# Experts in steps of 768, 1024 and 1024 inner columns instead of 256 and five times 512

## The chip, the core and the metric

The kernel runs on one core of a Trainium2 chip. Its time is the device time of one launch in microseconds (us), the median of three runs. TensorE does the matmuls, with a weight load (LDWEIGHTS) ahead of each; ScalarE (ACT), VectorE (DVE) and GpSimd (POOL) do the elementwise work; SyncE (SP) issues the weight loads from HBM to SBUF.

## What is computed

Four layers over 256 tokens of width 1024, all in float32. The first two are attention layers with a plain MLP, the third an attention layer with a gated MLP. The fourth ends in a mixture of eight experts, and only the expert part of it is rewritten by the change. For each expert, with the rows of the tokens that the router sent to it (up to 128 at a time here):

```
y = (silu(x @ w_gate) * (x @ w_up)) @ w_down     # gate, up: 1024 x 2816; down: 2816 x 1024
```

y is weighted by the router's share and added to the token's row; a final norm follows. Two experts are taken per token. The weights of the eight experts are 277 MB.

## The kernel before

**Products in three passes.** Every weight tile is split into a high part and a low part so that a float32 product comes out of three faster ones (line 2351: high by high, 2352: high by low, 2353: low by high). A tile comes into a **raw slot** of `slab` by two DMAs of SyncE (`tile`, line 626). ScalarE rounds it to its high part in `w_hi` (`hi`, line 1892), VectorE subtracts to get the low part in `w_lo` (`lo`, line 977), and TensorE uses both. A tile is 128 partitions by 2048 columns, 1 MB, and serves 12 matmuls of 512 columns. In the experts there are six raw slots and three **split slots** (slots 1 to 3 of the four in `w_hi` and `w_lo`; slot 0 stays free for the end). SyncE waits, before it loads a raw slot again, for VectorE's subtraction of what was in it (semaphore `lo_dve`). ScalarE waits, before it writes a split slot again, for TensorE's last matmul on what was in it (`w_used`). All queues are in order, and the order on each engine is written out by hand.

**An expert** has 33 tiles. Its 2816 inner columns are taken in `MS` = 6 steps: one of 256 columns (`narrow`), in which gate and up lie side by side in two tiles, and five of 512 columns, with two tiles for up, two for gate and two for down each. Rows of a gate or up tile are 1024 or 2048 bytes in HBM, those of a down tile 4096. In step j TensorE computes up into PSUM bank 1 and gate into bank 0, then does the down matmuls of step j-1 into banks 2 and 3 (`sums`), then transposes the hidden block of step j (`turn`, line 2470; four 128-column transposes). In between ScalarE takes silu of the gate bank (line 2279), VectorE multiplies by up (line 1757), and after the transposes ScalarE and VectorE split the turned block (lines 2179 and 1559). The sums of an expert's last step come in the next expert's step 0. ScalarE then scales them (`output`), and GpSimd scatters them with an add into `y_rows` in HBM; GpSimd also fetches the rows of the next expert (`fetch`), which TensorE transposes (`turn_fetched`, line 2841), and VectorE builds the list of the expert after (`lists`, `make_index`; two small products on line 2834).

The first expert's body and the last one's are written out, and a loop runs three times over two experts each (`each_expert`). Steps 2 to 4 of an expert are an inner loop.

**Ahead of the experts** lies the output projection of layer 4: four tiles, number 13 to 16 of that layer, in split slots 1, 2, 3 and 0. On ScalarE's queue behind it come, in this order:

```
ring.stage(3 if l < MOE else MORE_RAW, 3, 1)     # raw slots, split slots, first split slot
loads0 = list(ring.loads)
hi()
if l == MOE:
    hi()
...
    square_halves()                              # four squares with sums, line 1923
```

`stage` keeps in `last` which tile was last in each split slot, and `hi` waits for TensorE's use of that tile. The projection's result is added to x in four pieces by VectorE (`add_gated`, lines 1073 and 1074), each followed by ScalarE's square of that piece; VectorE computes the means in `cross_gated`, in the order add, add, add, `first_half(0)`, `first_half(1)`, `mean(0)`, add(1, 1), scaled row, `mean(1)`, scaled row. The means wait for the squares (`ss_done`), and the fourth square for the fourth add. Norm, router and the first gather of rows follow one after another.

Of the kernel before, what the change touches and what calls it, by code (L numbers as in the profile page):

```python
# [17 lines left out]
P = 128  # L18
D = 1024
# [47 lines left out]
F_WIDE = 512  # L67
# [22 lines left out]
X_MACT, X_MACT2, X_G, X_YE = 4096, 4864, 4608, 5376  # L90
# [114 lines left out]
def build(nc, A, out):  # L205
    ctx = ExitStack()
    with ctx:
# [10 lines left out]
        hT_lo = sb("hT_lo", [P, KC, SEQ], F32R)  # L218
        big = sb("big", [P, ADA])
# [13 lines left out]
        posi = sb("posi", [P, TT], I32)  # L233
# [7 lines left out]
        flag = sb("flag", [1, 1], I32)  # L241
# [77 lines left out]
        last_g, rows_out, rows_in = sem("last_g"), sem("rows_out"), sem("rows_in")  # L319
# [29 lines left out]
        MT = 3 * MJ  # L349
        MS = 1 + (FF2 - F_GATED) // F_WIDE  # L350

# [3 lines left out]
        def ff_tiles(l):  # L355
            return 4 * steps(l) if l < DEPTH else MT
# [165 lines left out]
        def expert_ring(ring, i, p, t0, loads0, ahead=2):  # L522


            done = MT * p + ahead
            ring.t, ring.i, ring.raw, ring.split = t0 + i * (2 * MT) + done, done, MORE_RAW, 3
            ring.at = 0 if isinstance(i, int) and i == 0 and p == 0 and t0 == ring.start else -MORE_RAW
            ring.loads = [c + i * (2 * MT // MORE_RAW) + sum(k % MORE_RAW == s for k in range(done))
                          for s, c in enumerate(loads0)]
# [10 lines left out]
        def expert_steps(eng, ring, step, before_last):  # L540

            with eng.Fori(0, MS - 3) as jj:
                ring.enter(jj, 6)
                step(jj + 2)
            ring.leave(MS - 3)
            before_last()
            step(MS - 1)

        def narrow(j):

            return isinstance(j, int) and j == 0

        def wide_at(j):

            return j * F_WIDE - F_GATED

        def expert_after(t0, loads0):

            return t0 + NE * MT, [c + NE * MT // MORE_RAW for c in loads0]
# [19 lines left out]
        def listed(p, b):  # L579

            return slice(KC // 2 * p + 2 * b, KC // 2 * p + 2 * b + 2)
# [5 lines left out]
        def by_two(src):  # L587

            return src.rearrange("p (a n) -> p a n", a=2)
# [4 lines left out]
        def _(sp):  # L594
# [82 lines left out]
            for l in LAYERS:  # L677
# [57 lines left out]
                else:  # L735
                    stage(MORE_RAW)

                    def expert_loads(t0, loads0, n0):
# [5 lines left out]
                        def body(i, p, n, first, last):  # L744
                            wg, wu, wd = weights(2 * i + p)
                            expert_ring(ring, i, p, t0, loads0)

                            def step(j, norm=False):
                                cols(wu, wide_at(j + 1), F_WIDE)
                                if norm:  # L750

                                    sp.wait_ge(sc_done, 2 * (UNIT0[l] + UNITS[l]))
                                cols(wg, wide_at(j + 1), F_WIDE)
                                if narrow(j):
                                    rows(wd, 0, 1)
                                else:
                                    rows(wd, 4 * j - 2, 2)

                            def final(j):
                                if not last:  # L760
                                    gated(*weights(2 * i + p + 1)[:2], 0)
                                rows(wd, 4 * j - 2, 2)

                            step(0, first and n0 == 0)
                            step(1)
                            if first and n0 == 0:
# [4 lines left out]
                            expert_steps(sp, ring, lambda j: final(j) if isinstance(j, int) else step(j), lambda: None)  # L771

                        ring.t, ring.i, ring.loads = t0, 0, list(loads0)
                        ring.at = 0 if t0 == ring.start else -MORE_RAW
                        gated(*weights(0)[:2], 0)
                        each_expert(sp, n0, body)

                    t0, loads0 = ring.t, list(ring.loads)
                    expert_loads(t0, loads0, 0)
# [3 lines left out]
                    with sp.If(full > P + 1):  # L783
                        expert_loads(*expert_after(t0, loads0), NE)
# [7 lines left out]
        def _(pool):  # L792
# [22 lines left out]
            with nc.allow_non_contiguous_dma(reason="256 positions"):  # L815
                pool.dma_start(posi[:, :].unsqueeze(2), A["positions_2"].rearrange("a (t p) -> p t a", p=P)).then_inc(v_in, 16)
# [92 lines left out]
            def clear_sums():  # L909

                pool.dma_start(y_rows.rearrange("(a p) d -> p a d", p=P), big[:, 0:D].unsqueeze(1).broadcast_to([P, TT + 1, D])
                               ).then_inc(scattered, 16)

            def fetch(p, n, n0):
# [3 lines left out]
                pool.indirect_dma_start(fetched, None, h_rows, bass.IndirectOffsetOnAxis(index[p][:, 0:1], 0)).then_inc(rows_in, 16)  # L918

            def scatter(p, n, n0):  # L920

                pool.wait_ge(yo_done, 2 * (n - n0 // NE) + 2)
                pool.wait_ge(scattered, 16 * (n + 1))
                pool.indirect_dma_start(y_rows, bass.IndirectOffsetOnAxis(index[p][:, 0:1], 0), y_out, None, compute_op=ALU.add  # L924
                                        ).then_inc(scattered, 16)

            def sums_back(turn_):

                pool.wait_ge(scattered, 16 * NE * (turn_ + 1))
                pool.dma_start(acc, y_rows[0:SEQ].rearrange("(t p) d -> p t d", p=P)).then_inc(acc_in, 16)  # L930

            def expert_rows(n0):

                for n in range(n0, n0 + NE):
                    p = n % 2
                    if n > n0:
                        scatter(1 - p, n - 1, n0)
                    if n < n0 + NE - 1:
                        fetch(1 - p, n + 1, n0)
# [4 lines left out]
            pool.wait_ge(rows_out, 32)  # L944
# [13 lines left out]
        def _(dve):  # L958
# [174 lines left out]
            def tables():  # L1133

                dve.wait_ge(v_in, 16 * V_LOADS)
                link(dve.tensor_copy(posf[:, :], posi[:, :]))
# [79 lines left out]
            for l in LAYERS:  # L1216
# [325 lines left out]
                if l >= DEPTH:  # L1542
                    ring.stage(3 if l < MOE else MORE_RAW, 3, 1)
# [152 lines left out]
                def matches(e, signal):  # L1696

                    pe_ = pos[:, :, bass.ds(e, 1)]
                    for t in range(TT):
                        dve.tensor_scalar(scr(X_G + t * P, P), iota, pe_[:, t], None, ALU.is_equal).then_inc(signal, 1)  # L1700

                def lists(e, n):
# [4 lines left out]
                    matches(e, g_done)  # L1707
# [12 lines left out]
                def last_lists(n):  # L1720

                    dve.wait_ge(ix_t, n + 1)
                    matches(NE - 1, last_g)

                def make_index(p, n, old):

                    dve.wait_ge(ix_t, n + 1)
                    if old:
                        dve.wait_ge(scattered, 16 * n)
# [1235 lines left out]
```

## Time and profile before

| what | value |
|---|---|
| median of the runs | 1911.68 us (1910.37, 1911.68, 1918.38) |
| span of the profiled execution | 1912.1 us, 0.4 us above the median |
| TensorE, ScalarE, VectorE busy | 1824.1, 1122.6, 1416.6 us |
| mean granted clock of TensorE | 0.983 of full speed |
| first expert's first matmul | 1142.61 us |
| last matmul on expert weights | 1896.70 us |
| DMA in the experts | about 381 GB/s |

The page names no time of the profiled execution apart from its span; the span is within the scatter of the runs and is taken as its own time. A matmul's duration in the rows is longer than the distance to the next one, since matmuls overlap; the pace is read from the starts. The clock is given as a share of 2.4 GHz: 1.00 is 2.4 GHz and 0.50 is 1.2 GHz.

### The profile page before, as it was taken

What the parts mean: (1) busy time and instruction counts of PE and PEld (TensorE: products, weight loads), DVE (VectorE), ACT (ScalarE), POOL (GpSimd) and SP (SyncE); (2) the same over time, 40 slices, a digit from 0 to 9 for tenths busy, and PEclk for the clock granted to TensorE, in tenths of its full rate; (3) what the DMA queues carried; (4) which work ended last, traced back from release to release, by engine and by line L of the source; (5) the groups of instructions that cost most, each with busy time, mean ns of one, the idle gap of its engine ahead of it and who ended that gap; (6) DMA issues with size and microseconds to landing.
All of it is one profiled execution on the core that took longest, in us unless ns stands there. A gap on an engine that the chain in (4) does not pass through costs nothing.

```text
span 1912.1 us, 26024 instructions
## 1 busy us (share of the span) xinstructions
PE 1824.1 (95%) x8799; PEld 1486.2 (78%) x8799; DVE 1416.6 (74%) x1631; ACT 1122.6 (59%) x1296; POOL 392.8 (21%) x315
## 2 busy tenths in 40 slices
PE   7899999989999998899989879999999999999997
PEld 6678886868888786688878667888888888888885
DVE  5748874466976586644458758889888888888897
ACT  6745444564443464443345537777777777777775
POOL 3722203463212363200046500000000000000000
PEclk9999999999999999999999989999999999999999
DMA  8348884418987341455544258999999999999994
GB/s 271 111 161 327 343 342 147 149 54 323 344 347 275 91 152 45 154 195 179 192 154 142 69 187 334 386 376 386 380 384 376 383 383 381 380 374 381 381 387 167
DMA packets 237934, 506.45 MB, mean 265 GB/s; under 512 B 23304, under 2 KB 74720, under 8 KB 231712
## 3 DMA queue, kind: packets, MB, share of 16 engines
q1 hardware_dynamic: 225664, 492.91, 70.9%
q0 software_dynamic: 3008, 10.32, 2.0%
q10 hardware_dynamic: 9184, 2.23, 0.5%
q8 instruction: 43, 0.70, 0.1%
q14 instruction: 35, 0.29, 0.0%
HBM read 497.49 MB, written 7.91 MB: 264 GB/s over the span
## 4 chain that ended last, share of the span: by engine, by line
PE 83%; DVE 7%; issue 6%; ACT 3%; POOL 1%; DMA 0%; POOLq 0%; SPq 0%; DVEq 0%; ACTq 0%
PE bank L2351 25%; PE bank L2353 25%; PE bank L2352 25%; PE bank L2470 2%; ACT slab L2042 1%; PE bank L2789 1%; DVE slab L1290 1%; PE bank L2561 1%; PE bank L2539 1%; ACT w_hi L1892 1%; PE bank L2521 1%; POOL w_lo L826 1%; DVE x L1074 0%; PE bank L2572 0%; DVE slab L1271 0%
## 5 line engine op out<-in xcount | busy, mean ns | idle before, releaser
L977 DVE TENSOR_TENSOR w_lo<-slab,w_hi 128x2048 fp32r<-128x2048 f32 x369 | 847.8, 2308 | 214.3 <-ACT w_hi L1892 213.3
L1892 ACT ACTIVATE w_hi<-slab 128x2048 fp32r<-128x2048 f32 (+2 forms) x421 | 796.6, 1898 | 329.0 <-PE bank L2353 256.3
L2351 PE MATMUL bank<-w_hi,hT_hi 128*128 128x512 f32 (+3 forms) x1664 | 649.4, 390 | 14.2 <-DVE hT_lo L1012 4.4
L2352 PE MATMUL bank<-w_lo,hT_hi 128*128 128x512 f32 (+3 forms) x1664 | 638.0, 383 | 0.0
L2353 PE MATMUL bank<-w_hi,hT_lo 128*128 128x512 f32 (+3 forms) x1664 | 637.9, 383 | 0.0
L2351 PEld LDWEIGHTS bank<-w_hi,hT_hi 128*128 128x128 f32 x1664 | 316.0, 190 | 77.9 <-DVE w_lo L977 8.8
L2353 PEld LDWEIGHTS bank<-w_hi,hT_lo 128*128 128x128 f32 x1664 | 315.5, 190 | 59.7
L2352 PEld LDWEIGHTS bank<-w_lo,hT_hi 128*128 128x128 f32 x1664 | 316.3, 190 | 55.3
L826 POOL TENSOR_TENSOR w_lo<-slab,w_hi 128x512 fp32r<-128x512 f32 (+2 forms) x208 | 262.4, 1295 | 381.3 <-ACT w_hi L1892 361.6
L2351 PE MATMUL bank<-w_hi,hid_hi 128*128 128x512 f32 x680 | 265.6, 391 | 0.7 <-DVE w_lo L977 0.7
L2353 PE MATMUL bank<-w_hi,hid_lo 128*128 128x512 f32 x680 | 265.0, 390 | 0.0
L2352 PE MATMUL bank<-w_lo,hid_hi 128*128 128x512 f32 x680 | 264.5, 389 | 0.0
L2351 PEld LDWEIGHTS bank<-w_hi,hid_hi 128*128 128x128 f32 x680 | 127.6, 188 | 29.2 <-issue 2.3
L2353 PEld LDWEIGHTS bank<-w_hi,hid_lo 128*128 128x128 f32 x680 | 127.6, 188 | 26.7
L2352 PEld LDWEIGHTS bank<-w_lo,hid_hi 128*128 128x128 f32 x680 | 127.7, 188 | 26.3
L924 POOL DMA_INDIRECT y_rows<-slab,posi x7 | 16.6, 2367 | 515.6 <-ACT slab L2263 515.6
L901 POOL TENSOR_TENSOR slab<-slab 128x512 f32<-128x512 f32 x32 | 60.0, 1893 | 251.6 <-ACT slab L2188 251.6
L1577 DVE SCALAR_TENSOR_TENSOR big<-slab,csilu,big 128x2048 f32<-128x2048 f32 x42 | 103.5, 2473 | 0.0
L2042 ACT ACTIVATE slab<-slab,att 128x256 f32<-128x256 f32 x144 | 71.4, 499 | 52.3 <-DVE att L1271 43.0
L2179 ACT ACTIVATE hid_hi<-bank 128x512 fp32r<-128x512 f32 (+1 forms) x95 | 47.6, 527 | 46.1 <-PE bank L2470 46.1
L1290 DVE TENSOR_TENSOR slab<-slab,att 128x512 f32<-128x512 f32 x56 | 52.7, 942 | 5.8
L1271 DVE CUSTOM_DVE_ANT_0 slab<-bank,const 128x256 f32<-128x256 f32 x88 | 31.9, 417 | 33.4 <-PE bank L2521 33.3
(252 smaller groups left out, 1232.0 us busy)
## 6 DMA issues: line engine op xcount, KB each, us to landing
slab<-in_w_exp_gate SPq DMA_DIRECT2D x176, 512.0 KB, 7.0
slab<-in_w_exp_up SPq DMA_DIRECT2D x176, 512.0 KB, 7.5
slab<-in_w_exp_down SPq DMA_DIRECT2D x176, 512.0 KB, 7.1
slab<-in_w_ada SPq DMA_DIRECT2D x48, 1024.0 KB, 5.5
slab<-in_w_mlp_in SPq DMA_DIRECT2D x64, 512.0 KB, 5.4
slab<-in_w_mlp_out SPq DMA_DIRECT2D x64, 512.0 KB, 9.0
slab<-in_w_in SPq DMA_DIRECT2D x56, 512.0 KB, 5.0
slab<-in_w_out SPq DMA_DIRECT2D x32, 512.0 KB, 4.6
```

The source lines that it names most:

```text
L826: ins = pool.tensor_tensor(w_lo[:, q, o], raw(s)[:, o], w_hi[:, q, o].bitcast(F32), ALU.subtract)
L901: pool.tensor_tensor(scr(X_ACT2 + t * F_UP, F_UP), a, a, ALU.mult).then_inc(sq_done, 1)
L977: dve.tensor_tensor(w_lo[:, q, 0:n], raw(s)[:, 0:n], w_hi[:, q, 0:n].bitcast(F32), ALU.subtract).then_inc(lo_dve, 1)
L1290: dve.tensor_tensor(p, p, r[:, s, :].unsqueeze(2).broadcast_to([P, TT, SEQ]), ALU.mult).then_inc(nrm_done, 2)
L1577: ins = dve.scalar_tensor_tensor(acc, w, c, acc, ALU.mult, ALU.add)
L1892: act.activation(w_hi[:, q, 0:n], raw(s)[:, 0:n], ACT.Copy).then_inc(hi_done, 1)
L2042: act.activation(p, p, ACT.Exp, bias=att[:, 1, j, t:t + 1], scale=-1.0, accum_out=att[:, 2, j, t:t + 1]).then_inc(ex_done, 1)
L2179: act.activation(to_hi[:, f0:f0 + n, t * P:(t + 1) * P], src, ACT.Copy).then_inc(hidh_done, 1)
L2351: pe.matmul(dst, a_hi, b_hi, start=start, stop=False)
L2352: pe.matmul(dst, a_hi, b_lo, start=False, stop=False)
L2353: return pe.matmul(dst, a_lo, b_hi, start=False, stop=stop_)
L2470: ins = pe.transpose(dst[t][:, f * P:(f + 1) * P], scr(src + t * width_ + f * P, P), ident)
```

## The change

The 2816 inner columns are taken in `MS` = 3 steps of 768, 1024 and 1024. Gate goes to banks 0 and 1, up to banks 4 and 5 (half of the step's columns in each bank, so 384 or 512 columns a matmul). A gate or up tile is now two rows of k by the whole step: 2 x 768 or 2 x 1024 columns, in HBM rows of 3072 or 4096 bytes. There are 36 tiles in an expert instead of 33: eight of 1536 columns, two of 1024 (the last two chunks of step 0's six down chunks), and 26 of 2048. TensorE's order within an expert is up and gate of step 0, down of the last expert's step 2, turn 0, up 1, gate 1, down 0, turn 1, up 2, gate 2, the turn of the fetched rows, down 1, turn 2. In the first expert up 1 comes ahead of turn 0 and uses banks 6 and 7. The split slots are all four, tile r in slot r % 4. Silu and the multiplication of a step are two instructions each, as are the two splits of the turned block. The inner loop is gone, the outer one stays. The list is in a part of scratch of its own, `hT_hi` and `hT_lo` each hold one expert's rows with high and low parts, the clearing of `y_rows` is three DMAs instead of one, and the waits count from constants instead of from the `Tiles` bookkeeping.

The core of the diff:

```
+E_WIDTH = (768, 1024, 1024)
+E_FROM = (0, 768, 1792)
+MS = len(E_WIDTH)
+MT = 36
...
+        def up_tile(j, first):
+            return (0 if first else -4, 8, 20)[j]
+        def gate_tile(j, first):
+            return (4 if first else 0, 12, 24)[j]
+        def down_tile(j):
+            return (4, 16, 28, MT - 4)[j + 1]
+        def tile_width(r, first, last):
+            if r in (18, 19):
+                return D
+            return 2 * E_WIDTH[0] if r < 4 or first and r < 8 or r >= MT - 4 and not last else TILE
...
+                        def wide_rows(w, j, n, r0):
+                            for b in range(4):
+                                to, loaded = slot_free(n, r0 + b)
+                                d = to[:, 0:2 * E_WIDTH[j]].rearrange("p (k n) -> p k n", k=2)
+                                for k in range(2):
+                                    sp.dma_start(d[:, k:k + 1, :], w[:, 2 * b + k:2 * b + k + 1, E_FROM[j]:E_FROM[j] + E_WIDTH[j]]
+                                                 ).then_inc(loaded, 16)
```

VectorE's queue in an expert:

```
+                        lows(2 if first else -1, gate_tile(0, first) + 7)
+                        activated(0)
+                        if first:
+                            lows(11, 15)
+                        else:
+                            lows(7, 11)
+                        hidden_low(0)
+                        if not last:
+                            lists(2 * i + p + 1, n + 1)
+                        lows(15 if first else 11, 19)
+                        activated(1)
+                        lows(19, 23)
+                        hidden_low(1)
...
+                            lows(23, 31)
+                        activated(2)
```

ScalarE ahead of the experts, and its rounding of a tile:

```
-                    ring.stage(3 if l < MOE else MORE_RAW, 3, 1)
+                    ring.stage(*((3, 3, 1) if l < MOE else (MORE_RAW, SPLIT, 0)))
                     loads0 = list(ring.loads)
-                    hi()
+                    hi(2 * E_WIDTH[0] if l == MOE else TILE)
                     if l == MOE:
-                        hi()
+                        hi(2 * E_WIDTH[0])
...
+                            def highs(r0, r1):
+                                for r in range(r0, r1):
+                                    w, s, q = tile_width(r, first, last), raw_slot(r), split_slot(r)
+                                    act.wait_ge(w_loaded[s], n * (32 * MT // MORE_RAW) + 32 * (loads0[s] + r // MORE_RAW + 1))
...
+                                    act.activation(w_hi[:, q, 0:w], raw(s)[:, 0:w], ACT.Copy).then_inc(hi_done, 1)
```

TensorE's queue in an expert:

```
+                        inner(0)
+                        gate(0)
+                        if first:
+                            inner(1)
+                            pe.wait_ge(ix_made, 2 * n + 2)
+                            turn(0)
+                        else:
+                            sums(-1)
+                            turn(0)
+                            inner(1)
+                        gate(1)
...
+                        sums(0)
+                        turn(1)
```

ScalarE's `highs`, silus and copies lie in the same places of its queue as VectorE's `lows`, `activated` and `hidden_low`. In the last expert four instructions that fold the scattered sums into x stand between VectorE's `lows` of tiles 24 to 28; before they stood between those of steps 3 and 4.

## Rows read from the trace of the kernel before

**Rows 1.** Busy time by stretch: each engine's us (instructions), granted clock, DMA share, GB/s.

```profile
1142.60:1146.80 4.20, 4.19 (x11) 3.33 (x12) 2.56 (x4) 2.21 (x2) 0.00 (x0) 0.60 0.14 53
...
1155.00:1217.00 62.00, 62.00 (x286) 51.40 (x285) 55.94 (x37) 44.81 (x29) 3.03 (x1) 1.00 1.02 381
1217.05:1310.78 93.73, 93.73 (x432) 77.76 (x431) 83.82 (x54) 70.63 (x49) 3.40 (x2) 1.00 1.04 381
...
1796.30:1896.90 100.60, 99.91 (x450) 81.15 (x448) 90.37 (x55) 70.85 (x50) 3.15 (x2) 1.00 0.88 328
```

**Rows 2.** Waits, 1200 to 1850 us: engine line <- awaited, us in total, times, longest.

```profile
ACT w_hi L1892 <- PE bank L2353: 93.2, 146, 1.2
```

**Rows 3.** Waits of SyncE's queue in the same stretch.

```profile
SPq L626 <- DVE w_lo L977: 375.0, 229, 3.1
```

**Rows 4.** Chain of work, 1100 to 1912 us: start, us, what.

```profile
1166.18 0.34 PE bank L2834 x4
...
1217.05 0.87 PE bank L2841 x8
...
1310.78 0.87 PE bank L2841 x8
```

**Rows 5.** TensorE in time order, 512-column matmuls: start, duration, line.

```profile
1293.14 0.39 PE L2353 MATMUL bank<-w_hi,hid_lo 128*128 128x512 f32 x1
...
1298.39 0.39 PE L2353 MATMUL bank<-w_hi,hT_lo 128*128 128x512 f32 x1
...
1309.95 0.39 PE L2353 MATMUL bank<-w_hi,hid_lo 128*128 128x512 f32 x1
```

**Rows 6.** TensorE in time order, 384-column matmuls of a projection.

```profile
712.42 0.33 PE L2351 MATMUL bank<-w_hi,hT_hi 128*128 128x384 f32 x1
...
715.71 0.33 PE L2352 MATMUL bank<-w_lo,hT_hi 128*128 128x384 f32 x1
```

**Rows 7.** ScalarE groups by form, whole run: busy us, mean ns.

```profile
L1892 ACT ACTIVATE w_hi<-slab 128x2048 fp32r<-128x2048 f32 x405 | 774.2, 1917 | 325.3 <-PE bank L2353 252.6 <-DMA slab<-in_w_mlp_in 55.9 <-DMA slab<-in_w_in 6.2
...
L1892 ACT ACTIVATE w_hi<-slab 128x1536 fp32r<-128x1536 f32 x12 | 17.6, 1488 | 0.0
```

**Rows 8.** Groups by form, 1280 to 1912 us: busy us, mean ns.

```profile
L977 DVE TENSOR_TENSOR w_lo<-slab,w_hi 128x2048 fp32r<-128x2048 f32 x216 | 492.6, 2291 | 62.8 <-ACT w_hi L1892 62.0 <-issue 0.3
...
L1757 DVE TENSOR_TENSOR slab<-slab,bank 128x512 f32<-128x512 f32 x33 | 22.5, 681 | 0.7
...
L2279 ACT ACTIVATE slab<-bank 128x512 f32<-128x512 f32 x33 | 19.8, 599 | 20.4 <-PE bank L2353 20.4
...
L1713 DVE TENSOR_TENSOR big<-big,rowg 128x1024 f32<-128x1024 f32 x2 | 2.4, 1218 | 0.0
```

**Rows 9.** The SyncE loads of line 626, 1217 to 1311 us: time from issue to landing.

```profile
DMA to landing us min/median/max: 4.9/7.6/9.8
```

**Rows 10.** ScalarE in time order, from the last projection to the first expert.

```profile
1096.62 1.90 ACT L1892 ACTIVATE w_hi<-slab 128x2048 fp32r<-128x2048 f32 x1
1103.40 1.92 ACT L1892 ACTIVATE w_hi<-slab 128x2048 fp32r<-128x2048 f32 x1 [4.88 <-PE bank L2353]
1110.31 0.63 ACT L1923 ACTIVATE h<-x 128x512 f32<-128x512 f32 x1 [4.99 <-DVE x L1074]
...
1115.67 0.63 ACT L1923 ACTIVATE h<-x 128x512 f32<-128x512 f32 x1 [1.99 <-DVE x L1074]
```

**Rows 11.** VectorE in time order, the last update of x.

```profile
1114.22 0.69 DVE L1073 TENSOR_TENSOR slab<-bank,rowg 128x512 f32<-128x512 f32 x1 [0.22 <-PE bank L2353]
1114.95 0.69 DVE L1074 TENSOR_TENSOR x<-slab,x 128x512 f32<-128x512 f32 x1
```

**Rows 12.** TensorE's last matmul of the output projection.

```profile
1113.80 0.39 PE L2353 MATMUL bank<-w_hi,hT_lo 128*128 128x512 f32 x1
```

**Rows 13.** TensorE in time order, its two waits in the first expert.

```profile
1150.90 0.44 PE L2470 MATMUL bank<-const,slab 128*128 128x128 f32 x2 [0.93 <-DVE slab L1757]
...
1154.57 0.50 PE L2351 MATMUL bank<-w_hi,hT_hi 128*128 128x512 f32 x1 [0.48 <-DVE w_lo L977]
```

More of the change, by code:

```diff
@@ L520, in build @@
         g_tables = rowg[:, 0:8 * HD].rearrange("p (a t d) -> p a t d", a=4, t=TT)
[L522 to L529, printed above, removed]
+        mact, mact2 = scr(X_MACT, max(E_WIDTH)), big[:, B_MACT2:B_MACT2 + max(E_WIDTH)]
+        EXPERT0 = FF0[MOE]
+        EXPERT_LO = FREE_RAW + EXPERT0 - len(POOLED)
         def each_expert(eng, n0, body):
@@ L742, in weights, with slot_free @@
                                     for n in ("w_exp_gate_2", "w_exp_up_2", "w_exp_down_2")]
[L744 to L766, printed above, removed]
+                        def slot_free(n, r):
+                            at = MT * n + r - MORE_RAW
+                            if at >= 0:
+                                sp.wait_ge(lo_dve, EXPERT_LO + at + 1)
+                            return raw(raw_slot(r)), w_loaded[raw_slot(r)]
@@ new lines, in expert_loads @@
+                        before = None
+                        for n in range(n0, n0 + NE):
+                            first, last = n == n0, n == n0 + NE - 1
+                            wg, wu, wd = weights(n - n0)
+                            wide_rows(wu, 0, n, up_tile(0, first))
+                            if n == 0:
+                                sp.wait_ge(sc_done, 2 * (UNIT0[l] + UNITS[l]))
+                            wide_rows(wg, 0, n, gate_tile(0, first))
+                            if not first:
+                                down_rows(before, -1, n)
+                            wide_rows(wu, 1, n, up_tile(1, first))
+                            wide_rows(wg, 1, n, gate_tile(1, first))
+                            down_rows(wd, 0, n)
+                            if n == 0:
@@ L770, in body @@
                                              ).then_inc(gfin_in, 16)
[L771 to L779, printed above, removed]
+                            wide_rows(wu, 2, n, up_tile(2, first))
+                            wide_rows(wg, 2, n, gate_tile(2, first))
+                            down_rows(wd, 1, n)
+                            if last:
+                                down_rows(wd, 2, n)
+                            before = wd
+                    expert_loads(0)
                     nrow += 1
@@ new lines, in activated @@
+                        def activated(j):
+                            at = ub + n * (2 * MS) + 2 * j
+                            banks = (bank[6], bank[7]) if first and j == 1 else (bank[4], bank[5])
+                            w = half_of(j)
+                            for c, o in enumerate(halves(j)):
+                                dve.wait_ge(act_done, at + c + 1)
+                                dve.tensor_tensor(mact2[:, o], mact[:, o], banks[c][:, 0:w], ALU.mult).then_inc(sq_done, 1)
@@ new lines, in turn @@
+                        def turn(j):
+                            nf = inner_chunks(j)
+                            banks = (bank[2], bank[3]) if first and j == 0 else (bank[0], bank[1])
+                            for f in range(nf):
+                                if f % (nf // 2) == 0:
+                                    pe.wait_ge(sq_done, ub + n * (2 * MS) + 2 * j + f // (nf // 2) + 1)
+                                src = mact2[:, f * P:(f + 1) * P]
+                                ins = pe.transpose(banks[f // 4][:, f % 4 * P:(f % 4 + 1) * P], src, ident)
+                            ins.then_inc(ht_done, 1)
```

421 lines of the change are left out of this document (225 added, 196 removed).

## The prediction

> **What bounds the kernel now.** I read the busy times by stretch first. In a whole expert, from one turn of fetched rows to the next, TensorE is busy 93.73 of 93.73 us at a granted clock of 1.00; VectorE is busy 83.82 us and ScalarE 70.63 [rows 1]. The chain of work has that turn at 1217.05 and again at 1310.78 us, so an expert costs TensorE's time to the hundredth [rows 4]. The DMA share of 1.04 looks like a second bound, so I read the waits: SyncE stands 375.0 us waiting for VectorE to free raw slots [rows 3], and ScalarE waits for TensorE to free split slots, 93.2 us in 650, never for a landing [rows 2]. A queue that is held back by its consumer is not what holds the consumer. TensorE sets the pace; the rest has to keep up.
>
> Next I took TensorE's pace apart. From 1298.39 to 1309.95 us there are 51 steps of 512 columns: 0.2267 us each [rows 5]. From 712.42 to 715.71 us there are 19 steps of 384 columns: 0.1732 us each, their weight loads included [rows 6]. The difference is 53.5 ns for 128 columns, 0.418 ns a column, so 12.6 ns of each matmul do not depend on its width. A transpose costs 0.87 / 8 = 0.109 us [rows 4]. From 1293.14 to 1298.39 us lie four transposes and 21 matmul steps: 5.25 - 21 x 0.2267 = 0.49 us, of which 0.44 are the transposes, so a break in the stream of matmuls costs 0.05 us beside its content [rows 5]. Check: 396 x 0.2267 + 30 transposes x 0.109 + 0.34 for the list [rows 4] + 6 breaks x 0.05 = 93.7 us, the period that was measured.
>
> **What the change does to an expert.** The columns stay the same. Step 0's up and gate are now 8 x 2 x 2 x 3 = 96 matmuls of 384 columns; the same work was 72 of 512. So 96 x 0.1732 - 72 x 0.2267 = 16.63 - 16.32 = +0.30 us. The turns go from six to three with the same 22 transposes; the fetched rows' turn, which adjoined a turn, now stands alone. Breaks go from six to four: -0.11 us. Together +0.19 us an expert, +1.5 us in eight.
>
> The rows put 12.6 ns on a matmul whatever its width. The Trainium skill ("TensorE: Matmul & The Clock Gate", Back-to-back issue gap) gives N/2.4 + 2.5 ns for an isolated warm matmul, 215.8 ns at 512 columns; the trace does not agree, with 226.7 ns. By its 2.5 ns the 24 extra matmuls would cost 0.06 us an expert and the sum would be 1.9 us lower.
>
> **Do the others still keep up?** Low parts first. A 1536-column subtraction has no row; between 1218 ns at 1024 and 2291 ns at 2048 columns [rows 8] I take 1755. VectorE then has 26 x 2.291 + 8 x 1.755 + 2 x 1.218 = 76.0 us in place of 33 x 2.291 = 75.6. On ScalarE 1488 ns at 1536 and 1917 at 2048 [rows 7] give about 1060 at 1024: 26 x 1.917 + 8 x 1.488 + 2 x 1.06 = 63.9 in place of 63.3. Products, copies and splits keep their number. Half a us more on engines with 10 and 23 us to spare costs nothing while their place in the queue is right, which has to be looked at apart.
>
> With three split slots a rounding starts when the tile three back is used, and its low part is there 1.92 + 2.29 = 4.2 us later, 1.2 us ahead of 2 x 2.72 us of matmuls (a tile is 12 x 0.2267 = 2.72 us). With four slots it is 8.2 - 4.2 = 4.0 us ahead. This margin pays for the longer interruptions. The tightest place in an ordinary expert is tile 23. Count from the end of tile 15: TensorE reaches tile 23 after 2 x 2.72 + 2 x 1.36 (the short down tiles) + 0.87 (eight transposes) + 0.34 (list) + 3 x 2.72 = 17.5 us. Rounding 21 starts when 17 is used, at 5.4; the low part of 21 is ready at 9.8, of 22 at 12.1; then the two halves of hidden_low, 1.36 by line 1757's 681 ns [rows 8]; the index, about 0.5; and tile 23 ends at 16.2. It is 1.3 us early. If it were late by d, d is paid in seven experts. In the last expert four folds of 1.22 us lie between tiles 24 and 28 and eat 4 x (1.22 + 2.29 - 2.72) = 3.2 us, so a wait of 1 to 2 us is due there; the last expert of before idles about as much (100.60 us against 99.91 busy, with slowed restarts) [rows 1]. I take zero, with 1.5 us both ways.
>
> Loads: slot r is loaded after the low part of tile r - 6. In the narrow stretch six tiles last 6 x 12 x 0.1732 = 12.5 us, rounding and subtraction 3.2, which leaves 9.2 us for a landing and 2.0 us of lead behind it: 11.2 us. Landings took 4.9 to 9.8 us, median 7.6 [rows 9]. Before it was 16.3 - 4.2 + 1.2 = 13.3. So nothing is paid, with a thinner margin. The fetch of the next expert's rows follows the index, at 13.9 us in the count above, and its turn comes behind gate 2, at 17.5 + 5 x 2.72 = 31.1; GpSimd's queue keeps its order and is 17 us early. The short DMAs of 256 and 384 KB and the six extra issues an expert lie in SyncE's waiting time [rows 3].
>
> **The first expert.** Before, TensorE waits 0.93 us for the product behind its first silu, with nothing else in the queue, and then 0.48 us for a low part whose rounding stood behind that silu [rows 13]. Now eight tiles and up 1 come before turn 0, and ScalarE rounds nine tiles before its first silu. TensorE has 10.9 us of matmuls over the silu (0.60 us each [rows 8]) even with a table load ahead. -1.4 us. If tiles 8 to 11 come late, because only six tiles of 1536 columns are in the raw slots at the start, up to 1 us of it stays.
>
> **The moved slot.** This is the largest term, and it is not in the experts. Expert tile 0 used to go into split slot 1, last used by projection tile 13; it now goes into slot 0, last used by tile 16, the final one. Before, ScalarE did the two roundings at 1096.62 and 1103.40 us, and was at the first square at 1110.31 [rows 10]. Now the first rounding waits for the last matmul of the projection, which starts at 1113.80 and takes 0.39 us [rows 12]: 1114.2. Everything queued behind it waits: rounding 0, rounding 1 (1.49 each [rows 7], less some 0.1 of overlap), then the squares from about 1117.0. VectorE waits for square 0 in `first_half(0)`, and behind that stand `mean(0)` and the fourth add. Three squares of 0.63 [rows 10] with about 0.1 each for reading out the sum end at 1119.2, `mean(0)` at 1119.4; the fourth add takes 1.42 us (1114.22 to 1115.64 [rows 11]) and ends at 1120.9; the fourth square starts there instead of at 1115.67 [rows 10]. That is +5.2 us on norm, router, gather and the first matmul, which follow one by one with no cover. From both sides: nothing, if something between the square and the gather waits for another thing; 6.8 us, if all four squares shift with the first (1110.31 to 1117.0).
>
> **Sum.** 1912.1 + 5.2 - 1.4 + 1.5 = 1917.4 us of span; against the median, 0.4 lower, 1917.0.
>
> **Rivals.**
> *The moved slot costs nothing* (chance 0.15). It needs an earlier release of slot 0 than I read. For: the rounding is only preparation. Against: the waits are in one queue ahead of the squares. Then 1917.0 - 5.2 = 1911.8.
> *The feed falls short in the narrow stretch* (0.18, slower). Eight tiles of 1536 columns fill six slots with a quarter less. For: the margin falls from 13.3 to 11.2 us, and the DMA share is already 1.04. Against: no landing of rows 9 was over 9.8. At 13.5 us each of seven experts pays 2.3 us: 1917 + 16 = 1933. It decides over slower by 0.5% from a landing of 11.8 us, 0.6 us an expert. Late low parts at tile 23 would look the same. The Trainium skill ("DMA: Bandwidth & Descriptors", Bandwidth) speaks for this rival with its rule to batch DMAs to 1 MiB; this trace moves 381 GB/s with DMAs of 512 KB, so the rule does not bind here before.
> *TensorE's clock falls once more* (0.05): TensorE now stands idle 5 us longer before the router. A stretch such as 1142.60 to 1146.80, at 0.60 granted, loses about 2 us over its matmuls [rows 1]: 1919, or 1921 with two.
> *Longer rows pay* (0.04, faster). If landings, not TensorE, set the pace in part, rows of 3072 and 4096 bytes would save time. TensorE's 93.73 of 93.73 speaks against it [rows 1]; a saving of 1.5 us an expert without the slot's cost gives 1900.
>
> **How the numbers follow.** The likeliest (0.58) has its own range of 1913 to 1921: the last expert 1.5 both ways, the start up to 1, the shift up to 6.8. To hold 8 in 10 the range goes down to 1909, over most of the first rival, and up to 1926, over the clock and the nearer part of the feed rival; beyond lie about 0.12 above and 0.06 below. A measurement of this kernel tells about 0.5% (9.6 us) from no change, so same is 1902 to 1921: 0.58 + 0.15 + 0.04 = 0.77. Slower, from the feed rival and a double clock loss, 0.18. Faster 0.05.
>
> **What would show it.** In the profile after: the rounding before the squares starts at about 1114.2 us on a wait for TensorE, the fourth square at about 1121, the first expert's matmul at about 1147.8; no wait of TensorE at its first turn; a period of 93.9 us between fetched turns with TensorE wholly busy; last expert as long as before within 1.5 us. The prediction is wrong if ScalarE shows waits for DMA in the experts, if TensorE waits for low parts in each expert, or if the squares start near 1110.

## The result, and the profile after

The changed kernel takes 1926.21 us (median of 4 runs, 1924.58 to 1927.95) against 1911.39 us: a ratio of 1.0067, 95% interval 1.0044 to 1.0089. Timed a second time it took 1922.2 against 1911.65, 1.0053 [1.0034, 1.0072]. It is slower both times. 1917.0 had been forecast, with a range of 1909 to 1926 and most of the chance given to a change within 0.5%: the first measurement lies 0.2 us above the range, the second inside it.

The head of its page:

```profile
span 1923.3 us, 25162 instructions
## 1 busy us (share of the span) xinstructions
PE 1830.4 (95%) x8991; PEld 1517.4 (79%) x8991; DVE 1415.1 (74%) x1653; ACT 1125.2 (59%) x1320; POOL 396.3 (21%) x317
```

The time of this profiled execution is named beside its span: 1925.05 us, 1.8 us more. By the same 1.8 us the profiled execution of before stood near 1913.9, some 2.5 us over the median of 1911.39, while this one stands 1.2 under its own. So of the 14.8 us between the medians the two traces show 11.2, the distance of the spans; the other 3.6 are scatter of single executions.

The chain of work shows the turns of the fetched rows, one an expert, which answer to [rows 4] (start, us, what):

```profile
1218.79 0.87 PE bank L2939 x8
1312.77 0.87 PE bank L2939 x8
1406.78 0.87 PE bank L2939 x8
1419.43 2.60 issue
1505.19 0.87 PE bank L2939 x8
1599.20 0.87 PE bank L2939 x8
1611.85 2.09 issue
1697.10 0.87 PE bank L2939 x8
1791.11 0.87 PE bank L2939 x8
```

Four of the six periods are 93.98 to 94.01 us. The other two are 98.41 and 97.90 us, and each of these holds a stretch in which TensorE waited for nothing that the profile shows. Busy time by stretch (first expert; ordinary; a long one; the last one; columns as in [rows 1]):

```profile
1146.53:1218.79 72.26, 72.26 (x344) 63.11 (x345) 63.74 (x46) 54.55 (x38) 2.27 (x1) 0.98 0.98 381
1218.79:1312.77 93.98, 93.98 (x456) 81.00 (x455) 83.60 (x57) 70.94 (x52) 4.45 (x2) 1.00 0.99 379
1406.78:1505.19 98.41, 95.81 (x456) 82.59 (x455) 83.76 (x57) 71.05 (x52) 4.39 (x2) 0.98 0.97 365
1791.11:1907.40 116.29, 116.26 (x555) 99.23 (x554) 102.67 (x65) 82.86 (x63) 2.39 (x2) 1.00 0.87 333
```

The long period has the same work (x456), 2.60 us idle and 1.8 us more of busy time. TensorE in time order there:

```profile
1418.39 1.04 PE L3019 MATMUL bank<-const,big 128*128 128x128 f32 x8
1422.03 0.44 PE L2453 MATMUL bank<-w_hi,hT_lo 128*128 128x384 f32 x1 [2.60 <-issue]
...
1423.00 0.33 PE L2455 MATMUL bank<-w_hi,hT_lo 128*128 128x384 f32 x1
...
1423.68 0.52 PE L2455 MATMUL bank<-w_hi,hT_lo 128*128 128x384 f32 x1
1424.00 0.52 PE L2453 MATMUL bank<-w_hi,hT_lo 128*128 128x384 f32 x1
```

The eight transposes are `turn(2)`, the last thing in the loop's body, and the 384-column matmul behind the wait is the first thing in it. So the wait is the branch back; three rounds have two of these. What is waited for there the trace doesn't name; the runs below show it. A microsecond and a half behind the wait the matmuls go from a pace of 0.173 us to 0.320, the pace of the clock's lower level, for ten of them: 10 x 0.147 = 1.5 us.

ScalarE ahead of the experts, which answers to [rows 10]:

```profile
1114.38 2.85 ACT L1958 ACTIVATE w_hi<-slab 128x1536 fp32r<-128x1536 f32 x2 [17.43 <-PE bank L2455]
1117.14 0.61 ACT L1989 ACTIVATE h<-x 128x512 f32<-128x512 f32 x1
...
1120.74 0.63 ACT L1989 ACTIVATE h<-x 128x512 f32<-128x512 f32 x1 [1.68 <-DVE x L1120]
```

Both roundings wait for the projection's last matmul, and the fourth square starts at 1120.74 instead of 1115.67. The waits in the experts of the changed kernel, 1200 to 1850 us (engine line <- awaited, us in total, times, longest):

```profile
ACT w_hi L2345 <- PE bank L2455: 117.8, 163, 3.4
...
PE bank L2453 <- issue: 4.7, 2, 2.6
ACT w_hi L2345 <- DMA slab<-in_w_exp_gate: 4.1, 3, 1.9
ACT w_hi L2345 <- DMA slab<-in_w_exp_down: 3.4, 5, 0.8
...
ACT w_hi L2345 <- DMA slab<-in_w_exp_up: 1.9, 3, 0.6
```

ScalarE now waits 9.4 us for landings, where [rows 2] had none, but TensorE's only waits are the two at the branch.

**Where the time went**, from trace to trace (first matmul on expert weights 1142.61 to 1146.53, last one 1896.70 to 1907.40): start +3.9; first expert, from its first matmul to the fetched turn, 74.44 to 72.26, -2.2; six periods 562.39 to 572.32, +9.9, of which 8.3 are the two branches (4.4 and 3.9 over the 94.0 of the others) and 1.6 the six times 0.27 of the others; from the last fetched turn to the last weight matmul 117.26 to 116.29, -1.0; behind it +0.5. Together +11.1, the spans differ by 11.2.

### The profile page after: what moved, and what is told of

Same layout as the page of the kernel before. It is cut to its first block, busy times and chain, and to the rows that moved or that the text cites. A ratio compares the mean times of both kernels' runs of the same rounds, so it can differ in the third digit from the quotient of the medians.

```text
span 1923.3 us, 25162 instructions
## 1 busy us (share of the span) xinstructions
PE 1830.4 (95%) x8991; PEld 1517.4 (79%) x8991; DVE 1415.1 (74%) x1653; ACT 1125.2 (59%) x1320; POOL 396.3 (21%) x317
## 4 chain that ended last, share of the span: by engine, by line
PE 83%; DVE 6%; issue 6%; ACT 3%; POOL 1%; DMA 0%; POOLq 0%; SPq 0%; DVEq 0%; ACTq 0%
PE bank L2453 25%; PE bank L2455 25%; PE bank L2454 25%; ACT slab L2108 1%; PE bank L2887 1%; DVE slab L1336 1%; PE bank L2568 1%; PE bank L2659 1%; PE bank L2637 1%; PE bank L3019 1%; ACT w_hi L1958 1%; PE bank L2619 1%; POOL w_lo L870 1%; PE bank L2670 0%; DVE x L1120 0%
## 5 line engine op out<-in xcount | busy, mean ns | idle before, releaser
L1788 DVE TENSOR_TENSOR w_lo<-slab,w_hi 128x2048 fp32r<-128x2048 f32 (+2 forms) x286 | 595.7, 2115 | 69.3 <-ACT w_hi L2345 66.7
L2453 PE MATMUL bank<-w_hi,hT_hi 128*128 128x512 f32 (+2 forms) x1352 | 516.9, 382 | 12.6 <-DVE hT_lo L1072 3.8
L2454 PE MATMUL bank<-w_lo,hT_hi 128*128 128x512 f32 (+2 forms) x1352 | 509.7, 377 | 0.0
L2455 PE MATMUL bank<-w_hi,hT_lo 128*128 128x512 f32 (+3 forms) x1336 | 503.7, 377 | 0.0
L1023 DVE TENSOR_TENSOR w_lo<-slab,w_hi 128x2048 fp32r<-128x2048 f32 x105 | 246.1, 2354 | 136.3 <-ACT w_hi L1958 136.3
L2454 PEld LDWEIGHTS bank<-w_lo,hT_hi 128*128 128x128 f32 x1352 | 257.7, 191 | 39.2
L2455 PEld LDWEIGHTS bank<-w_hi,hT_lo 128*128 128x128 f32 x1336 | 254.9, 191 | 41.1
L2455 PE MATMUL bank<-w_hi,hT_hi 128*128 128x512 f32 (+1 forms) x400 | 149.4, 374 | 0.0
L2453 PE MATMUL bank<-w_hi,hT_lo 128*128 128x512 f32 (+1 forms) x384 | 144.9, 377 | 4.7 <-issue 4.7
L2454 PE MATMUL bank<-w_lo,hT_lo 128*128 128x512 f32 (+1 forms) x384 | 143.7, 374 | 0.0
```

Source lines behind the costliest of these rows:

```text
L1023: dve.tensor_tensor(w_lo[:, q, 0:n], raw(s)[:, 0:n], w_hi[:, q, 0:n].bitcast(F32), ALU.subtract).then_inc(lo_dve, 1)
L1788: dve.tensor_tensor(w_lo[:, q, 0:w], raw(s)[:, 0:w], w_hi[:, q, 0:w].bitcast(F32), ALU.subtract).then_inc(lo_dve, 1)
L2453: pe.matmul(dst, a_hi, b_hi, start=start, stop=False)
L2454: pe.matmul(dst, a_hi, b_lo, start=False, stop=False)
L2455: return pe.matmul(dst, a_lo, b_hi, start=False, stop=stop_)
```

## The experiments

In the table, periods are those between fetched turns; "long" are the two with a branch. Ratios are to the kernel before on the same chip; its medians there were 1910.87 to 1911.68 us. The first matmul moves by several us between executions of code that is the same up to it ("both": 1142.65 and 1147.63), so it is read together with the distances inside a trace.

| run | median us | ratio [95%] | first expert matmul | periods, short; long |
|---|---|---|---|---|
| before | 1911.39 | | 1142.61 | 93.73; none |
| after | 1926.21 | 1.0067 [1.0044, 1.0089] | 1146.53 | 94.00; 98.41, 97.90 |
| after, again | 1922.2 | 1.0053 [1.0034, 1.0072] | 1147.81 | 94.00; 99.26, 96.41 |
| slot moved back | 1916.26 | 1.0025 [1.0013, 1.0037] | 1144.33 | 94.00; 96.31, 96.07 |
| loop written out | 1917.17 | 1.0030 [1.0018, 1.0042] | 1146.18 | 94.00; none |
| both | 1910.52 | 0.9996 [0.9981, 1.0012] | 1142.65 | 94.00; none |
| both, again | 1912.14 | 1.0002 [0.9989, 1.0015] | 1147.63 | 94.00; none |
| before, long body | 1927.27 | 1.0082 [1.0064, 1.0100] | 1147.40 | 93.73; 99.49, 98.71 |
| before, half long | 1911.21 | 0.9992 [0.9981, 1.0004] | 1139.78 | 93.74; none |
| before, slot moved | 1917.21 | 1.0019 [1.0004, 1.0035] | 1146.42 | 93.73; none |
| three slots, written out | 1922.51 | 1.0057 [1.0036, 1.0078] | 1142.34 | 95.25; none |
| both, short rows | 1913.84 | 1.0007 [0.9994, 1.0020] | 1140.12 | 94.00; none |
| both, step 0 packed | 1909.58 | 0.9992 [0.9981, 1.0003] | 1140.38 | 93.65; none |

**The slot moved back, in the changed kernel** (slot 1 first, as before; still four slots):

```
-            return r % SPLIT
+            return (r + 1) % SPLIT
-    ring.stage(... (MORE_RAW, SPLIT, 0) ...)      # in three places, and FREE_SLOT 0 -> 1
+    ring.stage(... (MORE_RAW, SPLIT, 1) ...)
```

> The changed kernel with its expert tiles in split slot (r + 1) % 4, so that the first tile follows projection tile 13 as before. If the moved slot is what delayed the start, ScalarE is at the first square near 1110.3 us again, the fourth square comes at about 1115.7 instead of 1120.7, and TensorE's first expert matmul at about 1142.6 instead of 1146.5: 3.9 us less, about 1922 us. If the late start has another cause (the order of the gather, the longer bodies), the first matmul stays near 1146.5 and the time near 1926. The long periods (98.4 and 97.9 us) should stay in either case.

ScalarE in time order:

```profile
1104.89 1.49 ACT L1958 ACTIVATE w_hi<-slab 128x1536 fp32r<-128x1536 f32 x1 [5.42 <-PE bank L2455]
1111.79 0.63 ACT L1989 ACTIVATE h<-x 128x512 f32<-128x512 f32 x1 [5.42 <-DVE x L1120]
...
1117.16 0.63 ACT L1989 ACTIVATE h<-x 128x512 f32<-128x512 f32 x1 [1.99 <-DVE x L1120]
```

The squares follow the additions again. This execution was about 1.5 us late already at the roundings (1104.89 against 1103.40), so the distance counts: from the projection's end to the first expert matmul 29.0 us, 28.8 before and 32.6 in the changed kernel. The time fell further than expected, to 1916.26: 5.9 us under the changed kernel's second measurement and 10.0 under its first. The branches are still there, as waits of 2.06 and 1.83 us, this time without a clock drop behind them:

```profile
1417.24 2.06 issue
...
1607.56 1.83 issue
```

**TensorE's loop over pairs of experts written out, in the changed kernel:**

```
-                    each_expert(pe, n0, body)
+                    for e in range(NE):
+                        body(e // 2, e % 2, n0 + e, e == 0, e == NE - 1)
```

> The changed kernel with TensorE's loop over pairs of experts written out, so that TensorE never branches back; the other engines keep their loops. If the waits of 2.6 and 2.1 us at 1419 and 1612 us are TensorE fetching the code it branches back to, both go, and the slow matmuls behind them: all periods 94.0 us, 8.3 us less, about 1918 us. If they come from another engine's loop or from data (the lists, the rows of the next expert), both stay and the time stays near 1926.

The fetched turns on both sides of the former first branch:

```profile
1406.44 0.87 PE bank L2939 x8
1500.42 0.87 PE bank L2939 x8
```

No wait for issue is left and all periods are 93.98 to 94.01; the median, 1917.17, is the expected one. The late start stays (fourth square 1120.40, 32.6 us from the projection's end to the first expert matmul).

**Both edits together.**

> Both edits in one kernel. If the two are the whole loss but for the narrower matmuls: 1926.2 - 3.9 - 8.3 = 1914, that is 2 to 3 us above the kernel before less what the first expert gains. If the edits don't add up, or something else was also slow, it stays above 1918.

> The kernel of e3_both again beside the other two, as their measure: 1910.5 us.

The kernel is level with the one before, twice, and some 3 us under the 1914 that was expected: the changed kernel's first median, from which that was worked out, was high. By the medians the slot costs 6.7 us (1917.17 less 1910.52) and the two branches 5.7 (1916.26 less 1910.52). Their sum over 1910.52 is 1922.9, which is what the changed kernel took the second time; the first time it took 3.3 more. This difference was not settled. The price of the branches varies from execution to execution (below), but it is not shown that this is the cause.

**The kernel before, with its inner loop written out** in TensorE's queue. The work is the same; the body of the outer loop grows from 504 matmuls on weights (the inner body counted once) to 792, each with its weight load:

```
-                        with pe.Fori(0, MS - 3) as j:
-                            ring.enter(j, 6)
+                        for j in range(MS - 3):
                             rows_up(j + 2)
                             sums(n, j + 1, False, False)
                             turn(j + 2)
```

> The kernel before, with TensorE's inner loop over steps 2 to 4 of an expert written out, so that the body of its outer loop has as many matmuls as in the changed kernel (396 an expert instead of 252), and nothing else changed. If the length of the code that is branched over makes the wait, two periods between fetched turns grow from 93.7 to about 98 us and the time rises by about 8 us to 1919. If the wait belongs to the new order of TensorE's work (only a short turn ahead of the branch) or to another engine, nothing changes: 1911.

TensorE in time order at the first branch:

```profile
1424.79 0.60 PE L2470 MATMUL bank<-const,slab 128*128 128x128 f32 x4
1429.27 0.50 PE L2351 MATMUL bank<-w_hi,hT_hi 128*128 128x512 f32 x1 [3.88 <-issue]
...
1430.28 0.63 PE L2352 MATMUL bank<-w_lo,hT_hi 128*128 128x512 f32 x1
1430.71 0.63 PE L2353 MATMUL bank<-w_hi,hT_lo 128*128 128x512 f32 x1
```

The wait appears in the kernel before, at 3.88 and 3.40 us, with a stretch at the lower clock behind it; the two periods are 5.8 and 5.0 us long. That is 10.7 of the 16 us that it lost. From trace to trace the rest is small: the first fetched turn comes 3.2 us later (1220.25 against 1217.05), and 3.2 + 10.7 is about the 13.7 between the spans (1925.8 against 1912.1). But 8 us had been expected, and all four executions lost 13.4 us or more against the median before. If the branches cost 10.7 us in each of them, 3 us or more are open.

**The same for one expert of the two**, a body of 648 matmuls on weights.

> The kernel before, with TensorE's inner loop written out for one of the two experts in the outer loop's body: 252 + 396 matmuls in it, between the 504 of before (no wait) and the 792 that waited. If TensorE keeps a fixed amount of code at hand and this still fits, the periods stay 93.73 us and the time 1911; if it doesn't, two periods are 4 to 6 us longer and the time is about 1920. Either way it tells where the limit lies. If instead the written-out loop itself were slow, each odd period would be longer.

No wait and no loss. So it is not the branch that costs but the length of what is branched over. With other engines' queues and the work the same, the limit lies between 648 and 792 matmuls with their weight loads; the changed kernel has 840. The DMA queue that carries instructions shows the same. Its lines for 1400 to 1800 us (packets, MB, share), first half long (before has the same line word for word), then long body, changed kernel, and changed kernel with the loop written out:

```profile
q8 instruction: 1, 0.02, 0.0%
```

```profile
q8 instruction: 19, 0.31, 0.3%
```

```profile
q8 instruction: 18, 0.29, 0.3%
```

```profile
q8 instruction: 16, 0.26, 0.3%
```

The line names no engine, but between before and the long body only TensorE's queue differs. A body that fits is hardly fetched again; one that doesn't is fetched all through, 16 KB at a time (0.29 MB in 18 packets, one in 22 us). The last line keeps one from reading too much into the packets: code without a branch back is fetched nearly as often, 16 packets, and TensorE waits for none of them. Only the fetch at the branch is waited for.

The Trainium skill ("Runtime: NRT & Kernel Launch", Instruction fetch mechanics) states the rule: instructions come in blocks of 16 KiB, 256 to a block, and a taken branch whose target is not in the window held at the moment waits for a fetch by DMA. The packets and the waits at the branch agree. It gives that window as two blocks, and TensorE's memory as 2048 instructions. With 648 matmuls and 648 loads a body of more than five blocks branches back for nothing, so two blocks is not the window of this engine; 792 and 792, 1584 instructions beside the transposes and register operations, miss it. More exactly the limit was not looked for.

**The kernel before, with the moved slot alone:** three split slots 0 to 2 instead of 1 to 3.

```
-    ring.stage(3 if l < MOE else MORE_RAW, 3, 1)
+    ring.stage(*((3, 3, 1) if l < MOE else (MORE_RAW, 3, 0)))       # in three places, and FREE_SLOT 0 -> 3
```

> The kernel before, with its expert tiles in split slots 0 to 2 instead of 1 to 3 (the free slot is then 3) and nothing else changed. The first tile then follows the projection's last tile. If the moved slot alone costs the late start, the first square is at about 1117 us, the fourth at about 1121, the first expert matmul 4 to 5 us later and the time 4 to 5 us longer, about 1915. If the cost needed the new experts as well, nothing changes.

```profile
1113.42 3.71 ACT L1892 ACTIVATE w_hi<-slab 128x2048 fp32r<-128x2048 f32 x2 [17.42 <-PE bank L2353]
...
1120.64 0.63 ACT L1923 ACTIVATE h<-x 128x512 f32<-128x512 f32 x1 [1.68 <-DVE x L1074]
```

ScalarE's rows are those of the changed kernel. The fourth square is 5.0 us late, the first expert matmul 3.8 (1146.42 against 1142.61). The median rose by 5.6 us; the ratio, 1.0019, stands for 3.6, with an interval of 0.8 to 6.7.

**The changed kernel again,** beside the last two.

> The changed kernel as it is, on the same chip as these: 1926 us as before, two periods between fetched turns of about 98 us. It is the measure for the other runs.

It took 1922.2 us where 1926 had been expected. The two waits are 3.42 and 2.15 us; behind the first 1.8 us more went to the lower clock, behind the second 0.3.

**Three split slots in place of four**, in the changed kernel with its loop written out:

```
-            return r % SPLIT
+            return 1 + r % 3          # and the counts of used slots: 3 in place of SPLIT
```

> The changed kernel with TensorE's loop written out, the first tile in slot 1, and three split slots (1 to 3) instead of four. By the margins worked out in the prediction a full tile is then ready 1.2 us before TensorE wants it, and two products or two splits in a row (1.36 us) use that up: TensorE should wait for low parts some tenths at several places of every expert, 1 to 2 us an expert, and the time should be 1919 to 1925. If four slots are more than it needs, the periods stay at 94.0 us and the time at 1911.

```profile
1243.94 0.47 PE L2453 MATMUL bank<-w_hi,hid_hi 128*128 128x512 f32 x1 [0.26 <-DVE w_lo L1788]
```

A period is 95.25 us (1214.15 to 1309.40 in the chain), 1.25 more: TensorE waits for low parts a few tenths at a time. Half of that is idle time (TensorE is busy 94.59 of the 95.25 us), the other half slower starts behind the waits: the same work takes 93.98 us in "both". The run compares with "both", which starts in slot 1 as well: 1.0057 against 0.9996 and 1.0002, some 11 us. So the fourth slot is needed, and its price is only that of where it lies.

**Short rows:** "both" with gate and up tiles in HBM rows of 1536 and 2048 bytes, half as long, each DMA of the same size.

```
-    for k in range(2):                                     # one row of k, the whole step
-        sp.dma_start(d[:, k:k + 1, :], w[:, 2 * b + k:2 * b + k + 1, ...step...])
+    for c, o in enumerate(halves(j)):                      # two rows of k, half the step
+        sp.dma_start(d[:, :, o], w[:, 2 * b:2 * b + 2, ...half of the step...])
```

> The kernel of e3_both with each gate and up tile loaded in halves of its columns, two rows of k at a time: the same two DMAs of the same size a tile, but HBM rows of 1536 and 2048 bytes in place of 3072 and 4096. If TensorE sets the pace and the longer rows are worth nothing here, periods stay at 94.0 us and the time at that of e3_both, 1910.5. If the longer rows carry part of the experts, landings come later, ScalarE waits for DMA and the time rises by several us.

ScalarE's waits for landings, 1200 to 1850 us, with short rows:

```profile
ACT w_hi L2346 <- DMA slab<-in_w_exp_down: 28.2, 32, 4.0
ACT w_hi L2346 <- DMA slab<-in_w_exp_gate: 15.4, 9, 2.2
ACT w_hi L2346 <- DMA slab<-in_w_exp_up: 2.0, 3, 0.8
```

and with long rows, in "both, again":

```profile
ACT w_hi L2345 <- DMA slab<-in_w_exp_down: 3.9, 4, 2.2
ACT w_hi L2345 <- DMA slab<-in_w_exp_gate: 2.0, 2, 1.1
```

Long rows do land sooner, and ScalarE waits 5.9 us for landings instead of 45.6 (12.7 in the first execution of "both"). Most of the waiting is for down tiles, whose rows are 4096 bytes in both. But the periods are 93.98 to 94.01 in both; TensorE sees none of it outside the last expert, where three more waits for low parts, of 0.26 to 0.39 us, appear. The times cannot be told apart.

**Step 0 packed:** "both" with gate and up of step 0 side by side in a tile of 1536 columns for one row of k, so that three matmuls of 512 columns do what four of 384 did.

```
+    for k in range(KC):                       # in TensorE's queue, in place of inner(0) and gate(0)
+        q = low_ready(up_tile(0, first) + k)
+        for c, dst in enumerate((bank[4], bank[5], bank[0 if first else 6])):
+            s = slice(c * COL, (c + 1) * COL)
+            ins = product(dst[:, :], ..., w_hi[:, q, s], w_lo[:, q, s], k == 0, k == KC - 1)
```

> The kernel of e3_both with step 0's gate and up packed: a tile is one row of k with 768 up and 768 gate columns, and TensorE does it as three matmuls of 512 columns into three banks instead of four of 384. This takes back the 24 extra matmuls of an expert. If a matmul costs 12.6 ns whatever its width, the period falls from 94.01 to 93.71 us and the time by 2.4 us, to about 1908, below both kernels. If a matmul's cost goes by columns alone, the period stays at 94.0.

```profile
1210.74 0.88 PE bank L2956 x8
...
1304.40 0.87 PE bank L2956 x8
```

The period falls to 93.65, 0.35 under that of the change, for 24 matmuls fewer an expert. This is the best time of all, 2.1 us under the kernel before by the median and 1.8 by the mean, and the interval still holds 1.

## Where the prediction was right and where it was wrong, point by point

- **What bounds the kernel**: right. TensorE is busy for the whole of each period but at the branches, and no wait for a landing or a low part reached it.
- **The moved slot, +5.2**: right in mechanism, and the largest term that was named. The rounding started at 1114.38 (1114.2 forecast), the fourth square 5.07 us late, at 1120.74 (1121). The first matmul came only 3.9 us late: behind the fourth square 1.2 us were caught up (1120.74 to 1146.53 is 25.79 us, 26.94 before; 25.78 in the kernel before with the slot moved). This was not cover but TensorE's clock. Up to the first of the small products that build the list the changed kernel fell 0.25 us further behind. These products were granted 0.89 instead of 0.50, which gave back 1.0 us, and the 32 that gather the rows 0.58 instead of 0.54, which gave back 0.4. "Both", with the slot where it was, needs 24.9 us for the same distance, with 0.70 in the gather. So the slot costs 5.0 us in the chain, and what the clock adds or takes there differs by 2 us between executions. The rival that it costs nothing has fallen.
- **Width of the matmuls, +0.19 an expert**: measured +0.27 with the turns' breaks. The +0.30 for the narrower matmuls is borne out by the packed kernel, which gains 0.35; of the 0.11 for fewer breaks 0.03 to 0.08 is left. By the 2.5 ns that the Trainium skill's page "TensorE: Matmul & The Clock Gate" (Back-to-back issue gap) gives for an isolated warm matmul packing would have gained an estimated 0.06; the measurement decides for the 12.6 ns of the rows.
- **First expert, -1.4**: -2.2. TensorE waits for nothing at its first turn. Before, the two waits took 1.9 us and not 1.4 when read from start to start, since the matmuls behind a wait start more slowly (0.32 to 0.34 us instead of 0.23). By the count of matmuls and transposes some 0.2 us of work moved past the fetched turn. The lower clock took as much as before, some 1.6 us (ten matmuls at half pace, eight before). **Last expert, 0 within 1.5**: -1.0, of which 0.7 is that TensorE idles 0.03 us in place of 0.69; the wait of 1 to 2 us that was worked out and then left out of the sum did not come.
- **The feed rival (0.18)**: fell, although a sign that was named for it came: ScalarE waits 9.4 us for landings, where the prediction had said that it is wrong if there are any. The sign was too strict, since none of these waits reached TensorE. Narrow tiles landed in 4.2 to 6.7 us (median), and the count of margins holds: it gave no wait with four slots, and with three, where it left a margin of 1.2 us, the wait came. **Longer rows pay (0.04)**: the rows land sooner and nothing is gained. **The clock falls once more (0.05)**: it did. Behind the idle time ahead of the norm, 7.15 us instead of 2.18, the sixteen transposes ran at 0.50, where the clock had been 1.00, but they cost no more than the 0.25 us above and ran as slowly with the slot moved back (3.61 us for the sixteen against 3.72). It also fell behind both branches, which the rival did not mean.
- **The step that failed is one sentence of the description that was priced at nothing: "The inner loop is gone, the outer one stays."** The sum counted an expert's matmuls, turns and breaks and multiplied by eight; it took a round of the loop as free and gave no reason; in the trace of before it was free, the period being TensorE's to the hundredth. But that was a body of 504 matmuls on weights, and the change makes it 840. It no longer stays at hand, and each branch back waits 1.8 to 3.9 us, with up to 1.9 us more at the lower clock behind it: 8.3 us in this profile. Written out, the wait is gone; made long in the kernel before, it appears; half as much longer, it does not. The range reached up to 1926 for the feed rival and for the clock, neither of which brought the time there; that the measured times end near its upper end is luck.
- **The baseline**: the span was taken for the execution's own time, which is 1.8 us more. This did no harm, since the distance to the median of 1911.68 grows by the same 1.8: 1917.4 + 1.8 - 2.2 is again 1917.0. With the terms as measured the sum of spans is 1912.1 + 3.9 - 2.2 + 9.9 - 1.0 + 0.5 = 1923.2, against 1923.3.

## What to carry to other kernels

Count the instructions between a loop's label and its branch, for each engine, before and after a change that removes an inner loop or makes steps longer: unrolling inside a loop can cost more than it saves; here a shorter body and no loop at all were both free of the wait. When a buffer slot is renumbered, look at who used the new slot last and at what stands behind the waiting instruction on its queue. A better feed (longer rows here) is worth nothing while the consumer holds it back, but the slots that keep it so have to be counted tile by tile.

## What the hardware showed that was not expected

- A taken branch on TensorE costs nothing visible with a body of 648 matmuls and as many weight loads, and 1.8 to 3.9 us from 792 on. The instruction queue's line tells whether a body is fetched again (1 packet in 400 us, or 18 and 19), but not whether TensorE waits: straight code has 15 or 16 packets in 400 us and no wait.
- The granted clock fell behind the wait in some executions (after 2.60 and 2.09 us in the changed kernel, some 1.8 us lost each time) and not in others (2.06 and 1.83 us with the slot moved back; 2.15 in the changed kernel again), so the length of the wait alone does not decide it; a branch cost 2.1 to 5.8 us in all.
- With the same code ahead of the experts the first expert matmul came at 1139.78 us in one execution and 1147.40 in another (half long and long body, which differ behind it alone). Distances inside a trace are sounder than starts.
- At the same DMA size and much the same rate (384 and 380 GB/s), rows of 4096 bytes instead of 2048 brought the median landing of up and gate loads of 512 KB from 8.4 and 9.7 us to 7.9 and 8.2 over 1217 to 1311 us. Down loads, whose rows stayed as they were, landed sooner as well, after 7.1 instead of 9.1 us. The first line is short rows, the next long ones:

```profile
slab<-in_w_exp_gate SPq DMA_DIRECT2D x16, 512.0 KB, 9.7
```

```profile
slab<-in_w_exp_gate SPq DMA_DIRECT2D x16, 512.0 KB, 8.2
```
